# Paired 64x64 inverse products, earlier table loads and a shorter router in a hybrid trunk kernel

## The reference

```python
# RWKV-7, one direction; the kernel does it in chunks of 64 tokens with a 64x64 inverse per head
sa = einsum('bhvk,bhk->bhv', S, kkt)
S = S * wt[:, :, None, :] - sa[..., None] * bt[:, :, None, :] + vt[..., None] * kt[:, :, None, :]

o = concatenate([o_att, o_rw, o_ssd], -1)
x = x + g1 * (o @ w_out)                       # out-projection, 8 feature tiles of 128
h = rmsnorm(x, norm2_w) * (1 + sc2) + sh2
scores = sigmoid(h @ router_w); sel = scores + router_bias
grp = top_k(sel.reshape(-1, 4, 4), 2)[0].sum(-1)        # best group of 4, by its two best experts
g_idx = argmax(grp, -1)
_, e_idx = top_k(where(in_grp, sel, -inf), 2)           # two experts of that group
```

## Time and profile before

| | |
|---|---|
| median of 3 runs | 1091.25 us (1085.15, 1091.25, 1092.33) |
| the profiled execution | 1087.14 us, span of its records 1085.3 us |
| TensorE busy | 978.2 us (90% of the span) |
| VectorE busy | 483.0 us (45%) |
| ScalarE busy | 307.1 us (28%), 41 table loads of 1.28 us in it |
| granted TensorE clock, mean | 0.973 |
| DMA | 238.74 MB, 220 GB/s over the span |

### The profile page before, as it was taken

One profiled execution on the slowest core, in us unless ns is written; L12 is line 12 of the kernel. 1 busy time (PEld: TensorE's weight loads), 2 busy tenths in 40 slices (PEclk: granted clock), 3 DMA queues, 4 the chain that ended last, 5 costly groups with the idle time before them and its releaser, 6 DMA issues. The chain is left out here.

```text
span 1085.3 us, 25550 instructions
## 1 busy us (share of the span) xinstructions
PE 978.2 (90%) x11105; PEld 705.0 (65%) x11105; DVE 483.0 (45%) x1371; ACT 307.1 (28%) x661; POOL 51.5 (5%) x79
## 2 busy tenths in 40 slices
PE   6899998988879989979989998899888999997786
PEld 4555566788758865645745565778876976664355
DVE  1362388567731343212546156746873252311134
ACT  2330417332221710110153132733322251111000
POOL 0000000000000020012000000000000002000120
PEclk9899999999999999999999999999999999999899
DMA  9759533422168759999742204232027756999993
GB/s 382 304 152 273 157 109 126 157 81 86 66 241 363 293 195 400 378 366 396 318 161 78 77 5 156 88 148 81 8 86 315 306 194 242 393 380 351 381 416 87
DMA packets 43447, 238.74 MB, mean 220 GB/s; under 512 B 5120, under 2 KB 8192, under 8 KB 19904
## 3 DMA queue, kind: packets, MB, share of 16 engines
q1 hardware_dynamic: 29904, 196.37, 47.0%
q0 software_dynamic: 9584, 34.35, 10.5%
q10 hardware_dynamic: 3840, 6.29, 1.8%
HBM read 210.25 MB, written 26.74 MB: 218 GB/s over the span
## 5 line engine op out<-in xcount | busy, mean ns | idle before, releaser
L1030 PE MATMUL bank<-sb_hT,sb_ring 128*128 128x385 f32 (+1 forms) x640 | 206.7, 492 | 4.4 <-ACT sb_hT L1698 4.4
L1030 PEld LDWEIGHTS bank<-sb_hT,sb_ring 128*128 128x128 f32 (+1 forms) x640 | 115.3, 187 | 90.9 <-issue 10.2
L1030 PE MATMUL bank<-sb_arena 64*64 64x64 f32 (+5 forms) x1048 | 102.1, 333 | 9.2 <-DVE sb_arena L2612 3.6
L1698 ACT ACTIVATE sb_u<-bank 128x256 f32<-128x256 f32 (+4 forms) x106 | 48.7, 476 | 204.5 <-PE bank L1030 195.3
L1030 PE MATMUL bank<-sb_ring,sb_arena 128*64 128x256 f32 (+4 forms) x672 | 91.2, 401 | 16.4 <-PEq L1652 10.5
L1030 PE MATMUL bank<-sb_o,sb_ring 128*128 128x257 f32 (+1 forms) x512 | 84.9, 327 | 1.6 <-DVE sb_o L2041 0.9
L1030 PEld LDWEIGHTS bank<-sb_ring,sb_arena 128*64 128x64 f32 (+2 forms) x672 | 56.1, 154 | 44.8 <-issue 33.9
L1030 PEld LDWEIGHTS bank<-sb_o,sb_ring 128*128 128x128 f32 x512 | 77.4, 190 | 10.0 <-issue 2.8
L1030 PEld LDWEIGHTS bank<-sb_arena 128*64 128x64 f32 (+2 forms) x1048 | 58.9, 141 | 35.2 <-issue 22.6
L2041 DVE SCALAR_TENSOR_TENSOR sb_xT<-bank,sb_mod,sb_xT 128x128 f32<-128x128 f32 x144 | 41.1, 345 | 82.3 <-PE bank L1030 81.9
L1030 PE MATMUL bank<-sb_u,sb_arena 64*64 64x64 f32 (+2 forms) x744 | 62.4, 315 | 7.9 <-DMA sb_u<-weights 3.9
(11 more groups left out here) (217 smaller groups left out, 1257.3 us busy)
## 6 DMA issues: line engine op xcount, KB each, us to landing
sb_ring<-weights SPq DMA_DIRECT2D x110, 1024.0 KB, 6.9
sb_arena<-weights SPq DMA_DIRECT2D x37, 1024.0 KB, 20.0
sb_u<-weights SPq DMA_DIRECT2D x18, 1024.0 KB, 12.3
sb_sq<-weights SPq DMA_DIRECT2D x8, 1024.0 KB
sb_hT<-weights SPq DMA_DIRECT2D x8, 1024.0 KB
x_slots<-sb_o POOLq DMA_DIRECT2D x1, 6912.0 KB, 39.4
sb_sq<-x_slots POOLq DMA_DIRECT2D x18, 256.0 KB, 7.6
sb_hT<-x_slots POOLq DMA_DIRECT2D x17, 256.0 KB, 7.7
```

What stands on the lines that cost most here:

```text
L1030: return nc.tensor.matmul(out, lhsT, rhs, start=start, stop=stop, skip_group_check=True)
L1698: return nc.scalar.activation(out, in_, func, **kw)
```

## The change

Six edits. In the diff `...` marks what is left out.

1. The two batches of a pair now go through each step together. `sixteen` issues the products of both batches in turn; the second batch keeps its `inv` with the two 64-partition halves swapped, so that its products go from the lower partitions to the upper rows of its bank and the reverse. In place of an add of a product to `inv`, the second batch multiplies with (1 + power) and ScalarE copies the result; the merges do the same for both batches, by masks with the identity in them. Each step waits for both batches.
2. Loads of ScalarE's tables are issued by hand, ahead of use, and Ln and Exp share one table (`roots_next`).
3. The router has fewer VectorE operations; `lgT` is made before the transposes `hm`; three `keep_warm` before the second half of `lg` are gone.
4. `gathered` is cut into two pairs of blocks, the second behind `turn(0)`, each with 128 columns; `picks` are made in two halves.
5. `out_projection` begins with features 0 to 5 of the first two output tiles, before `mix_ready`, in place of five `keep_warm`.
6. Waits for both batches of a chunk before the recurrence's `values`.

```diff
-            out += [(step, first), (step, first + 1)] + SSD_BESIDE.get((first, step), [])
+            out += [(step, first)] + SSD_BESIDE.get((first, step), [])
...
+            def sixteen(banks_, at, lhsT, rhs, turned=(0, 1)):
+                for j in range(4):
+                    last = []
+                    for m in range(2):
+                        for i, q in enumerate(HALVES):
+                            out = HALVES[(i + turned[m]) % 2]
+                            ins = mm(banks_[m][out, at + 64 * j:at + 64 * j + 64], lhsT[m][q, j, :], rhs[m][q, j, :])
+                        last.append(ins)
+                return last
...
+                    if k == 1:
+                        pe.wait_ge(matrices_ready, len(RW_BATCHES) * l + b + 2)
+                    if k < 4:
+                        banks_ = [open_bank(pe, "p", l, m, k) for m in pair[::-1]]
+                        if k > 1:
+                            taken(pe, "p", l, b, k - 1)
+                        last = sixteen(banks_, 256, pw[::-1], pwT[::-1], (1, 0))
+                        if k < 3:
+                            last = sixteen(banks_, 0, pwT[::-1], pw[::-1], (1, 0))
...
+                    if k > 1:
+                        banks_ = [open_bank(pe, "t", l, m, k) for m in pair]
...
+                            pe.wait_ge(powers_plus_one, len(RW_BATCHES) * l + b + k - 1)
+                        if k > 2:
+                            for m in pair:
+                                taken(pe, "t", l, m, k - 1)
+                        for ins in sixteen(banks_, 0, [pwT[0], pwT[1] if k == 4 else cross[1]], inv):
+                            ins.then_inc(psum_filled, 1)
...
+                elif step == "merge0":
...
+                    for ins in sixteen(banks_, 0, [invT[m] for m in pair], cross):
...
+                    for m in range(2):
+                        eight(banks_[m], 0, cross[m], invT[pair[m]]).then_inc(psum_filled, 1)
...   ScalarE, steps of the pair
+                    elif k < 3:
+                        for m in (1, 0):
+                            if k == 2 and m == 0:
+                                filled(act, "t", l, b, 2)
...
+                            copy(power[m].rearrange("p k j n -> p (k j) n"), "p", l, b + m, k)
+                    if k > 1:
+                        copy(inv[1], "t", l, b + 1, k)
...   VectorE
+                    for i, q in enumerate(HALVES):
+                        last = tt(inv[1][HALVES[1 - i]], power[1][q, 0, :, :], bc(C("ident64", q), 1, 4), ALU.add)
...
+                    for m in pair:
+                        left = g4[m][:, :, 2, :]
+                        tt(left, left, one, ALU.add).then_inc(cross_left_ready, 1)
...
+                    if k < 4:
...
+                        tt(cross[1], power[1][:, 1, :, :], one, ALU.add).then_inc(powers_plus_one, 1)
...
+            def roots_next():
+                nc.scalar.preload_act_table_set("natural_log_exp_and_others")
...
+                banks_ = [open_bank(pe, "out", l, n, 0) for n in range(OUT_AHEAD)]
+                taken(pe, "pv", l, 2)
+                pe.wait_ge(rw_mix_ready, l + 1)
+                for n, bank in enumerate(banks_):
+                    if n % 2 == 0:
+                        items_.append(next_item())
+                    add_features(bank, n, 0, range(SSD_FEATURES))
+                pe.wait_ge(mix_ready, l + 1)
+                for n, bank in enumerate(banks_):
+                    add_features(bank, n, 0, range(SSD_FEATURES, KT)).then_inc(psum_filled, 1)
-                        if n + half == 0:
-                            keep_warm(bank, 5)
...
-                    if half:
-                        keep_warm(bank, 3)
...
-                gathered()
+                gathered(0)
                 used = blocks_used(pe, l)
                 gate_up(0)
                 for b in range(STORED):
                     if b + 1 < STORED:
                         gate_up(b + 1)
                     turn(b)
+                    if b == 0:
+                        gathered(1)
...   ScalarE, end of second_norm; then in moe lgT before hm, and Silu's table behind hm
+                nc.scalar.preload_act_table(ACT.Sigmoid)
...   VectorE, routing: five operations for the groups' sums in place of nine
+                tt(rt[:, 3, 0:24], ones_of, twos_of, ALU.max)
+                link(tt(rt[:, 4, 0:24], ones_of, twos_of, ALU.add))
+                tt(rt[:, 5, 0:12], pairs(3)[:, :, 0], pairs(3)[:, :, 1], ALU.add)
+                link(tt(rt[:, 6, 0:12], pairs(4)[:, :, 0], pairs(4)[:, :, 1], ALU.max))
+                link(tt(small4(7), small4(5), small4(6), ALU.max))
...
-                link(v.tensor_copy(inside, bc(small4(9), 3, 4)))
```

More of the change, by code:

```diff
@@ L352, in psum_plan @@
         g("a", "lg", l, 1)
+        g("a", "lgT", l)
         for t in range(TILES):
@@ L360, in psum_plan @@
         fill(l, "rows")
-        for k in range(KT // 2):
-            g("a", "xp", l, k)
+        for k in range(2):
+            g("a", "xp", l, 0, k)
         g("v", "gu", l, 0)
@@ L367, in psum_plan @@
             g("v", "hT", l, b)
+            if b == 0:
+                for k in range(2):
+                    g("a", "xp", l, 1, k)
             if b + 2 >= GATHERED:
@@ L1366, in recurrence_step @@
                     bank = open_bank(pe, "rv", l, q)
-                    taken(pe, "tt", l, batches[1], 1)
+                    for d in range(2):
+                        taken(pe, "tt", l, batches[d], 1)
                     for j in range(4):
@@ L1512, in moe @@
                     last.then_inc(psum_filled, 1)
+                bank = open_bank(pe, "lgT", l)
+                taken(pe, "lg", l, 1)
+                tr(bank[:, 0:32 * TILES], logits, 32 * TILES).then_inc(psum_filled, 1)
                 for t in range(TILES):
@@ L1930, in moe @@
                     f(logits[rows, :], bank[rows, 0:P], ACT.Copy).then_inc(read("lg", l, half), 1)
+                bank = filled(act, "lgT", l)
+                f(shaped(rt[:, 1, :], TILES, 16), shaped(bank[:, 0:32 * TILES], TILES, 32)[:, :, 0:16],
+                  ACT.Sigmoid).then_inc(read("lgT", l), 1)
                 for t in range(TILES):
@@ L1949, in copy_tokens, with gathered @@
                     f(turned_at(b), shaped(bank[:, :], KT, SLOT), ACT.Copy).then_inc(read("xb", l, b), 1)
-                for k in range(KT // 2):
-                    bank = filled(act, "xp", l, k)
-                    for i in range(2):
-                        last = f(xbT[:, :, 2 * k + i, :], shaped(bank[:, i * 256:(i + 1) * 256], GATHERED, SLOT), ACT.Copy)
-                    last.then_inc(read("xp", l, k), 1)
+                def gathered(pair):
+                    for k in range(2):
+                        bank = filled(act, "xp", l, pair, k)
+                        f(xbT[:, 2 * pair:2 * pair + 2, 4 * k:4 * k + 4, :].rearrange("p b c s -> p c b s"),
+                          shaped(bank[:, :], 4, 2, SLOT), ACT.Copy).then_inc(read("xp", l, pair, k), 1)
                 def store_block(b):
@@ L2322, in ssd_step, with matrices @@
                     last.then_inc(read("hst", l), 1)
[L2324 removed]
+            def matrices(l, b):
                 d = RW_BATCHES[b][1]
                 s = b % 2
[L2328 to L2344 removed]
@@ new lines, in matrices @@
+                for half in range(2):
+                    bank = filled(dve, "g4", l, b, half)
+                    mask = bc(bc(C(f"rw{d}"), 1, 2), 1, 2)
+                    tt(g4[b].rearrange("p j (a k) n -> p j a (k n)", k=2)[:, half::2, :, :],
+                       shaped(bank[:, :], 2, 2, P), mask, ALU.mult)\
+                        .then_inc(read("g4", l, b, half), 1)
+                for half in range(2):
+                    bank = filled(dve, "nd", l, b, half)
+                    tt(power[s][:, 0, half::2, :], shaped(bank[:, 0:P], 2, 64), bc(C(f"nd{d}"), 1, 2), ALU.mult)\
+                        .then_inc(read("nd", l, b, half), 1)
@@ new lines, in inverse_step, with four @@
+            def inverse_step(l, step, b):
+                pair = (b, b + 1)
+                one = bc(C("ident64"), 1, 4)
+                def four(bank, at=0):
+                    return shaped(bank[:, at:at + 256], 4, 64)
+                if step == "matrices":
+                    for m in pair:
+                        matrices(l, m)
+                    dve.wait_ge(matrices_ready, len(RW_BATCHES) * l + b + 2)
+                    for m in pair:
+                        left = g4[m][:, :, 2, :]
+                        tt(left, left, one, ALU.add).then_inc(cross_left_ready, 1)
@@ L2345, in inverse_step @@
                 elif step[:5] == "power" and step != "power1":
                     k = int(step[-1])
+                    if k < 4:
+                        if k == 3:
+                            filled(dve, "t", l, b + 1, 2)
+                        taken(dve, "p", l, b + 1, k - 1)
```

(5 more changed lines are left out.)

314 lines of the change are left out of this document (163 added, 151 removed).

## The result

| | before | after |
|---|---|---|
| median | 1090.75 us (13 runs, 1084.08 to 1092.70) | 1097.77 us (13 runs, 1090.91 to 1102.13) |
| ratio | | 1.0071, 95% interval 1.0051 to 1.0090 |
| profiled execution, span | 1085.3 us | 1095.1 us |
| TensorE busy | 978.2 us | 949.7 us |
| mean granted clock | 0.973 | 0.949 |

The kernel became 7.7 us slower (0.7%), within 1% of before, where 20 us faster was forecast. TensorE is busy 28 us less and yet the end comes later: what was saved in work was more than lost again in waits.

A forecast was written before the change was run, and what follows sets the result against it. It took TensorE and VectorE, both nearly full, to bound the inversion and the weights' stream the expert stage. Terms 6 + 0.25 + 1 + 5.8 + 5.9 = 19 from 1087.1 gave 1068, 1072 against the median; forecast 1070, range 1055 to 1090.

The forecast's parts named there:

- Inversion, what is removed: Inversion: paired records drop from 29 to 21 ns, saving 3.3 us of TensorE per pair; bounds nothing to 6.7 us.
- a rule for neighbours in one bank: Inversion: neighbouring records writing different banks take 12 ns, one bank 28; half of sixteen's steps change bank, hence 21 ns.
- the bound of 13: Inversion: fast limit of 13 ns a paired record, 6.7 us per pair, 18 us in all.
- Inversion, what is added: Inversion: joint waits and added VectorE and ScalarE work leave a net gain of 3 us per layer, 6 in all.
- rival (d): Inversion: TensorE idles more and its clock falls to the 1.2 GHz level, 36 us for two layers, 1106 us; chance 0.07.
- my own chain for pair 2: Inversion, hand-made order of pair 2: little cover, loses 0.7 us, idle time going from 1 to 3.5.
- Out-projection ahead: Out-projection: starts 1.9 us earlier in layer 0, 0.7 in layer 1; 1 us gained in all, bounds -0.6 and 2.6.
- The half price taken for the lower clock: Out-projection's start: without keep_warm four records at the lower clock cost 1.6 us more; half of it was counted.
- Router and tables: Router: pos starts 2.9 us earlier per layer, 5.8 in all; table loads: 0.25 us at layer 1's first norm.
- Gathering: Gathering and experts: gathered(0) takes 5.4 us, gate_up(0) comes 5.9 earlier, the experts' stream gains 5.9 in all; bounds 0 and 11.8.
- rival (b): Experts: their stream doesn't start with the gathering, its total sets the end; the 5.9 falls away, 1076 us; chance 0.12.
- the likeliest case: Whole kernel: the forecast itself, all terms as summed, 1070 us; chance 0.46.

The follow-up runs named there:

- w_serial: w_out_warm with the loops of sixteen turned round, all eight products of one batch and then the other's; 1083.04 us, 0.9969, 4.9 us slower than w_out_warm.
- rest_only: Kernel before with edits 2 to 5 and without the pairing; 1086.41 us, 0.9994 to before.
- tab_router: Kernel before with edits 2 and 3 alone (tables, router); 1081.86 us, 0.9929 to before, 7.7 us faster.
- pair_tr: Kernel before with edits 1, 2, 3 and the waits of edit 6, no added keep_warm; 1085.87 us, 0.9977 to before.
- pair_tr_out: pair_tr with edit 5 (out-projection ahead) added, no added keep_warm; 1090.56 us, 1.0028 to before, 5.6 us over pair_tr.
- w_out_warm: warm4 with four keep_warm more ahead of out-projection's first product; 1080.02 us, 0.9924 to before, the fastest kernel of the study.
- warm4: Changed kernel with four keep_warm in the wait ahead of power1 of each pair; 1083.51 us, 0.9947 to before.
- inv_warm: Kernel before with edit 1 (pairing, with its waits) alone and four keep_warm ahead of power1; 1092.49 us, 1.0075 to before.
- w_gath_back: warm4 with edit 4 undone, all four blocks gathered in one go with 256 columns; 1084.81 us, 0.9973 to before, 2.8 us over warm4.
- before_warm: Kernel before with two keep_warm in its wait ahead of power1 of each pair's second batch, the control for warm4; 1089.77 us, 0.9998 to before.

## Why the prediction was wrong, point by point

**Inversion, what is removed.** Forecast 21 ns a record from a rule for neighbours in one bank; measured 14.7, near the bound of 13. TensorE saved 416 x 14.3 = 5.9 us a pair. (In the working, (0.65 - 0.22)/16 is 27 ns and not 28; nothing hangs on it.) The step was wrong in size and in mechanism, and on the good side: not the step between banks but the number of quadrants at work sets the rate, as the starts of the records show. The Trainium skill (TensorEngine Tiling, section Gotcha 1: PSUM Pressure) says that different row tiles can't access one bank at the same time, and I took the 0.41 and 0.65 us of the earlier trace rows as agreeing. The traces differ: in the kernel before, records of the lower and the upper rows start 7 ns apart for one bank.

**Inversion, what is added.** This is the step that failed. "The step matrices is set by VectorE; nothing changes there" overlooked that power1 of the first batch filled half of that time. The wait grew from 1.24 to 2.9 to 3.4 us in five of six pairs, and TensorE's idle time in the two stages from 15.8 to 44.3 us. With it came the second error: the drop of the clock stood as rival (d) with 0.07, argued away with "single waits there are 1.24 us", the waits of the kernel before and not those of the changed one, though my own chain for pair 2 had idle time going to 3.5. Behind a 2.70 us wait the rows already showed 0.50, and single waits of 1.24 us weren't all that before had: the one of 2.31 us in layer 1, with 0.59 behind it, was overlooked. Forecast 6 us faster; measured 5.2 to 8.4 slower on four bases. The price that (d) named, 36 us with all of TensorE's work there at the lower level, was too high: the mean clock of the two stages was 0.88 and 0.87. How much of the loss is the clock and how much the waits themselves isn't settled. The Trainium skill, TensorEngine Tiling, section PSUM Bottleneck, warns that tiling speeds TensorE and not the emptying of the banks; the runs agree in that w_serial shows 16 us of TensorE's time worth only 5.

**Out-projection ahead.** In layer 0 the start came nearly as forecast, 1.7 us sooner, with a wait for weights of 2.10 us; in layer 1 of the changed kernel it came 1.4 later. The half price taken for the lower clock was too low: 4.7 and 5.6 us slower on two bases, where 1 faster was forecast and the bound was 0.6 slower. I priced four records behind the wait (1.6 us); in rest_only the clock was below full for some 10 us (0.66 on the mean), 3.1 us to the logits in layer 0.

**Router and tables.** Right. 2.9 us a layer forecast for `pos`; 3.0 and 2.3 in the profiles, by the step named (TensorE's keep_warm ends last, `pos` has no wait). With tables 6.05 us forecast, 7.7 measured (4.8 to 10.7). In tab_router's own profile this stretch is shorter by 3.0 us in layer 0 and by only 0.6 in layer 1, so part of the 7.7 isn't accounted for by this step.

**Gathering.** The front came as forecast: 5.62 for 5.4 us, and in kernels without the late copy `gate_up(0)` starts 5.8 us sooner. Passing it on was wrong: the stream resumed 7.6 us sooner, but then shared the engines with the token loads, which in tab_router had run in that idle time (273 against 429 GB/s at full share). In its effect that was rival (b), given 0.12, though not by (b)'s way, in which the stream doesn't start sooner.

**The sum.** Forecast -6 -0.25 -1 -5.8 -5.9. By the runs, adding the edits one after the other (tab_router, pair_tr, pair_tr_out, the changed kernel): router and tables -7.7, pairing +5.2, out-projection +5.6, gathering +4.7, together +7.8, the +7.7 measured. On the other bases the last three came out at 6.1 to 8.4, at 4.7 and at -2.8 to 2.8. The fall of the clock, the joint waits and the end of the experts that doesn't move were all named somewhere in the prediction, and the likeliest case was the one in which every cover held.

## What to carry to other kernels

Joining two independent chains in lockstep takes away each other's cover: before pricing cheaper instructions, write down for each new joint wait what ran in it, above all in the first step, which "doesn't change". Where TensorE's waits grow to the length of those behind which the profile already shows the lower clock, price what follows at that level for as long as the rows show it last, or fill the wait (four products in each, 2.8 us, gave back 13.5 us in the changed kernel, but 2.9 and nothing on two other bases, so try it on yours). Before removing keep_warm, look at the clock behind it. Where a stream is to start sooner, ask what other transfers will then run beside it. And try small edits alone first, as two of six carried all the gain.

## What the runs showed of the hardware

64x64 float32 products take 29 ns a record with two quadrants of the array at work and 14.7 with four (two banks in turn); batch after batch, with the four at work for part of the time, they take 18. A quadrant takes a record in 58 ns in all of them, and records of the lower and the upper rows start 7 ns apart though they go to one bank. In this stage TensorE also shows waits inside one group of products that nothing in the profile ends: 3.46 us at 267.64, others near 1.0 us; in before the longest are 2.28 and 2.31. For layer 1's stage they sum to 4.6 us in w_out_warm, 7 in warm4 and inv_warm, 8.2 in the changed kernel and 11.1 in w_gath_back, against 4.1 in before and 2.9 in before_warm. In 263 to 266, ahead of the longest, the DMA share was 0.98; whether instructions came late was not tried. And DMA engines at a busy share of 1.0 moved anything from 273 to 431 GB/s: 429 and 431 with weights alone (packets of 8 KB, 310 ns each), 273 to 314 with packets of 4 KB from the token loads beside them.
